# A first stage whose sums go to VectorE and whose first panel runs chunk by chunk, and third panels split earlier

## What is computed

```python
for l in range(DEPTH):
    mod = silu_c @ w_ada[l] + b_ada[l]
    sh_a, sc_a, g_a, sh_f, sc_f, g_f = jnp.split(mod[:, None, :], 6, axis=-1)
    ...
    hx = rmsnorm(x) * (1 + sc_a) + sh_a
    hc = rmsnorm(ctx) * (1 + mc[1]) + mc[0]
    ux = hx @ w_in[l]
    ...
    x = x + g_a * (jnp.concatenate([fx, ax, rx], axis=-1) @ w_out[l])
    x = x + g_f * swiglu(rmsnorm(x) * (1 + sc_f) + sh_f, w_gate[l], w_up[l], w_down[l])
```

## Time and profile before

| | |
|---|---|
| runs of the kernel before, us | 3932.67, 3937.05, 3923.95 (median 3932.67) |
| the profiled execution, its own time | 3933.46 us |
| its span in the profile | 3932.2 us |
| mean granted TensorE clock | 0.96 |
| PE busy | 3710.9 us (94%) |
| DVE busy | 1800.4 us (46%) |
| ACT busy | 1170.1 us (30%) |
| line 389, low halves of 260 panels, DVE | 595.2 us, 2291 ns each |
| line 384, high halves of 260 panels, ACT | 495.3 us, 1907 ns each |
| from main memory | 335.95 MB, 86 GB/s over the span |

### The profile page before, as it was taken

One profiled execution on the slowest core, in us unless ns is written; L12 is line 12 of the kernel. 1 busy time (PEld: TensorE's weight loads), 2 busy tenths in 40 slices (PEclk: granted clock), 3 DMA queues, 4 the chain that ended last, 5 costly groups with the idle time before them and its releaser, 6 DMA issues.

```text
span 3932.2 us, 46910 instructions
## 1 busy us (share of the span) xinstructions
PE 3710.9 (94%) x20048; PEld 3027.0 (77%) x20048; DVE 1800.4 (46%) x2365; ACT 1170.1 (30%) x1511; POOL 144.3 (4%) x122
## 2 busy tenths in 40 slices
PE   7989889999999888999999999799999999999998
PEld 5866678888887566788788877578887888777886
DVE  3125655222243367433454456654446445466444
ACT  3125333111132253322332233442223223223222
POOL 1000210000000012000000002000000000000000
PEclk9999799999999998999999999899999999999999
DMA  6414201111111100222322222022222222222221
GB/s 246 161 71 162 88 33 55 64 65 65 65 65 65 71 3 31 89 97 97 118 86 97 97 97 73 26 96 97 97 98 96 97 97 107 86 86 78 99 98 59
DMA packets 47757, 341.06 MB, mean 87 GB/s; under 512 B 5392, under 2 KB 5552, under 8 KB 7744
## 3 DMA queue, kind: packets, MB, share of 16 engines
q1 hardware_dynamic: 41184, 301.09, 21.3%
q0 software_dynamic: 5216, 34.88, 2.3%
q10 hardware_dynamic: 1152, 2.10, 0.1%
HBM read 335.95 MB, written 2.10 MB: 86 GB/s over the span
## 4 chain that ended last, share of the span: by engine, by line
PE 88%; DVE 6%; ACT 2%; issue 2%; POOL 1%; DMA 1%; DVEq 0%; ACTq 0%; POOLq 0%
PE PS L412 52%; PE PS L430 18%; PE PS L414 7%; PE PS L1038 2%; PE PS L1054 1%; PE PS L1093 1%; DVE nmax_a L1188 1%; PE PS L1335 1%; PE PS L516 1%; DVE SQ L553 1%; PE PS L713 1%; PE PS L1068 1%; PE PS L1626 1%; PE PS L505 0%; PE PS L644 0%
## 5 line engine op out<-in xcount | busy, mean ns | idle before, releaser
L389 DVE TENSOR_TENSOR WL<-raw,WH 128x2048 fp32r<-128x2048 f32 x260 | 595.2, 2291 | 299.9 <-ACT WH L384 299.8
L384 ACT ACTIVATE WH<-raw 128x2048 fp32r<-128x2048 f32 x260 | 495.3, 1907 | 575.3 <-PE PS L412 346.6
L412 PE MATMUL PS<-XH_ff,WH 128*128 128x512 f32 x640 | 254.3, 397 | 6.9 <-DVE WL L389 6.9
L412 PE MATMUL PS<-XL_ff,WH 128*128 128x512 f32 x640 | 252.3, 394 | 0.0
L412 PE MATMUL PS<-XH_ff,WL 128*128 128x512 f32 x640 | 251.4, 393 | 0.0
L2024 DVE TENSOR_TENSOR GA_ff<-PS,GA_ff 128x512 f32<-128x512 f32 (+1 forms) x63 | 36.0, 599 | 334.5 <-PE PS L414 222.4
L412 PE MATMUL PS<-XH_a,WH 128*128 128x512 f32 x448 | 174.3, 389 | 0.0
L412 PE MATMUL PS<-XL_a,WH 128*128 128x512 f32 x448 | 174.3, 389 | 0.0
L412 PE MATMUL PS<-XH_a,WL 128*128 128x512 f32 x448 | 174.3, 389 | 0.0
L412 PE MATMUL PS<-XH_b,WH 128*128 128x512 f32 x448 | 174.3, 389 | 0.0
L412 PE MATMUL PS<-XL_b,WH 128*128 128x512 f32 x448 | 174.3, 389 | 0.0
(11 more groups left out here) (414 smaller groups left out, 8377.4 us busy)
## 6 DMA issues: line engine op xcount, KB each, us to landing
raw<-in_panels SPq DMA_DIRECT2D x260, 1024.0 KB, 4.7
ada_at<-in_ada_panels SPq DMA_DIRECT2D x24, 1024.0 KB, 4.8
ada_win<-in_ada_panels POOLq DMA_DIRECT2D x18, 1024.0 KB, 5.1
ada_start<-in_ada_panels POOLq DMA_DIRECT2D x6, 1024.0 KB, 22.5
FX<-in_dft_x POOLq DMA_DIRECT2D x2, 2048.0 KB, 8.2
X<-in_xT SPq DMA_DIRECT2D x1, 3072.0 KB, 11.2
out<-X ACTq DMA_DIRECT2D x8, 256.0 KB, 2.0
rope<-in_rope POOLq DMA_DIRECT2D x2, 768.0 KB, 10.2
```

Source lines behind the costliest of these rows:

```text
L384: H.up(ac.activation(WH[s].rearrange("p k n -> p (k n)"), raw[:, n % 2, :], ACT.Copy), n)
L389: L.up(ve.tensor_tensor(WL[s].rearrange("p k n -> p (k n)"), raw[:, n % 2, :], WH[s].bitcast(F32).rearrange("p k n -> p (k n)"), ALU.subtr ...
L412: t = te.matmul(PS[:, j, :], lhsT, x[:, k, 0:SEQ], start=st, stop=end)
```

## The change

It has three parts.

1. **The start.** Raw panel 0 is asked for first, then X in four transfers of two chunks each, then raw panel 1; POOL asks for the ada panels only when the first quarter of X has landed. ScalarE and VectorE split panel 0 before the squares. The squares are summed on VectorE (`ve_square_sum`) instead of TensorE. TensorE does root, spread and the first four ada panels ahead of panel 0, with the root in bank 0 and the spread in banks 2 and 3. Panel 1 is split behind the root.
2. **Panel 0 chunk by chunk.** `te_first` goes over the chunks k and in each over both blocks; ada panels 4 to 7 of the start stand between the chunks. VectorE's copies and additions for them are spread over the loop of `ve_normed`, which scales chunks 4 and 6 after the low half of the chunk ahead. The sixteen other ada panels are spread over panels 1 to 8.
3. **The entries.** In ff0, wi1 and ff1 the third panel is split right behind the normed chunks, ahead of the first panel's results. The second panel's split stands behind the root. `bias_sum` stands behind `te_root`, at k = 1, and uses bank 4.

The core of the diff (signals, plain renaming of banks and the same edits in the other engines' programs are left out):

```diff
@@ -114,7 +114,7 @@
...
 SPLITS = split_steps()
-ENTERED = entered_stages() | {FIRST["ff0.up0"], FIRST["wi1"], FIRST["ff1.up0"]}
+ENTERED = entered_stages() | {0} | {FIRST[name] + p for name in ("ff0.up0", "wi1", "ff1.up0") for p in range(2)}
...
@@ -366,6 +366,8 @@
...
                 panel_landed[n % 2].up(sp.dma_start(raw[:, n % 2, :], panels[n]), n)
+                if n == 0:
+                    sp_x()
...
@@ -418,6 +420,27 @@
...
                     beside(p, 2)
+        def te_first(name, XH, XL, ready, beside, evac):
+            p0 = FIRST[name]
+            for k in range(NC):
+                beside(k)
+                ready(k)
+                for j in range(2):
+                    if k == 0:
+                        te.wait_ge(*L[p0])
+                        wait_bank(j)
+                        wait_bank(2 + j)
+                    for q, (w, x) in enumerate(((WH, XH), (WH, XL), (WL, XH))):
+                        st, end = k == 0 and q == 0, k == NC - 1 and q == 2
+                        lhsT = w[0][:, k, j * P:(j + 1) * P]
+                        te.matmul(PS[:, j, :], lhsT, x[:, k, 0:SEQ], start=st, stop=end)
+                        t = te.matmul(PS[:, 2 + j, 0:CTX], lhsT, x[:, k, SEQ:TOK], start=st, stop=end)
+                    if k == NC - 1:
+                        B.up(t, (name, j))
+                        evac(j, j)
+            B.mark(("panel", p0))
...
@@ -554,9 +577,10 @@
...
+            late = (4, 6) if ahead else ()
             scale(0)
             for c in range(NC):
-                if c + 1 < NC:
+                if c + 1 < NC and c + 1 not in late:
                     scale(c + 1)
...
@@ -564,6 +588,10 @@
...
                     V.up(t, (name, "XL", c))
+                    if after:
+                        after(c)
+                    if c + 1 in late:
+                        scale(c + 1)
                     if c + 2 < NC:
...
@@ -622,11 +650,10 @@
...
                 te.wait_ge(*A[(name, "bias parts")])
-                wait_bank(5)
                 for j in range(2):
-                    t = te.matmul(PS[:, 5, 2 * j:2 * j + 2], RS[:, j * P:(j + 1) * P], HM[:, 2:4], start=True, stop=True)
+                    t = te.matmul(PS[:, 4, 2 * j:2 * j + 2], RS[:, j * P:(j + 1) * P], HM[:, 2:4], start=True, stop=True)
                 T.up(t, (name, "bias"))
-                bank(5, V, name, "bias")
+                bank(4, V, name, "bias")
...
@@ -654,10 +681,9 @@
...
                 T.up(t, (name, "raw", k))
-                if k == 0:
-                    bias_sum()
                 if k == 1:
                     te_root(name, norm_ctx)
+                    bias_sum()
                 if k == (2 if ctx else 3):
...
@@ -668,22 +694,24 @@
...
             A.up(ac.activation(RS[:, 0:2 * P], PS[:, 4, 0:2 * P], ACT.Copy), (name, "bias parts"))
-            for q in SPLITS[FIRST[run]]:
-                ac_split(q)
-            ac_stats(name, norm_ctx, False)
+            ac_stats(name, norm_ctx, False, between=SPLITS[FIRST[run]])
...
             ac_normed(name, XH, norm_ctx, shift, free)
+            for q in SPLITS[FIRST[run] + 1]:
+                ac_split(q)
         def ve_enter1(name, run, XH, XL, norm_ctx, gain, shift):
+            ve_stats(name, norm_ctx)
             ve.wait_ge(*T[(name, "bias")])
-            V.up(ve.tensor_copy(shb[:], PS[:, 5, 0:4]), (name, "bias"))
-            ve_stats(name, norm_ctx)
+            V.up(ve.tensor_copy(shb[:], PS[:, 4, 0:4]), (name, "bias"))
             for q in SPLITS[FIRST[run]]:
...
             ve_normed(name, XH, XL, norm_ctx, gain, shift)
+            for q in SPLITS[FIRST[run] + 1]:
+                ve_split(q)
...
@@ -752,39 +780,39 @@
...
         ada_use = {}
-        plans = {2: ("P0", "S0 P1", "S1 P2", "S2 P3", "S3")}
-        def ada_steps(start, rounds, p, j):
-            x = 2 * (p % 2) + j
-            if (j == 2 and x != 4) or p // 2 >= 4:
+        def ada_steps(p, j):
+            x = 2 * p + j - 2
+            if p == 0 or j == 2:
                 return []
-            return [(what[0], int(what[1]), start + (p // 2) * 2 * rounds + int(what[1]))
-                    for what in plans[rounds][x].split()]
-        def te_ada(name, b, start, rounds):
+            if x == 0:
+                return [("P", 0), ("P", 1)]
+            if x == 1:
+                return [("S", 0), ("S", 1), ("P", 2)]
+            return [("S", x)] + ([("P", x + 1)] if x + 1 < MOD // 2 - NC else [])
...
@@ -798,67 +826,118 @@
...
             cvec_landed.up(sp.dma_start(cv[:], cvec))
-            x_landed.up(sp.dma_start(X[:, :, :], xT))
+        def sp_x():
+            for i in range(4):
+                x_landed[i].up(sp.dma_start(X[:, 2 * i:2 * i + 2, :], xT[:, 2 * i:2 * i + 2, :]))
...
             const_landed.up(gp.dma_start(HM[:], head_mask), "all")
+            gp.wait_ge(*x_landed[0].now())
             for s, panel in enumerate(START):
...
             A.up(ac.activation(cv[:], cv[:], ACT.Silu), "cv")
+            ac_split(0)
             ac.wait_ge(*A["cv"])
             A.up(ac.activation(sh[:], cv[:], ACT.Copy, scale=0.0))
-            ac.wait_ge(*x_landed.now())
             ac.wait_ge(*V["consts"])
             for c in range(NC):
-                if c >= 2:
-                    ac.wait_ge(*T[("wi0", "sum", c - 2)])
-                A.up(ac.activation(SQ[c % 2][:, 0:TOK], X[:, c, :], ACT.Square), ("wi0", "square", c))
-            ac_stats("wi0", True, True)
+                if c % 2 == 0:
+                    ac.wait_ge(*x_landed[c // 2].now())
+                if c >= 3:
+                    ac.wait_ge(*V[("wi0", "square", c - 2, "added")])
+                A.up(ac.activation((SQ[c % 2] if c else SS)[:], X[:, c, :], ACT.Square), ("wi0", "square", c))
+            ac_stats("wi0", True, False, RS, 0, 2, SPLITS[0])
...
             V.up(ve.memset(one[:], 1.0), "consts")
+            ve_split(0)
+            for c in range(1, NC):
+                ve_square_sum("wi0", ("wi0", "square", c), c % 2, TOK, c == 1)
+            ve_stats("wi0", True)
+            ve_start_copy(0)
+            ve_start_copy(1)
             ve.wait_ge(*const_landed["all"])
-            for s in range(2):
-                ve_ada_parts("st", START[s], mix1[0]["AD"], s)
-            ve_stats("wi0", True)
-        def ve_start_chunks(c):
+            ve_start_bias(0)
+            ve_start_bias(1)
+            for q in SPLITS[0]:
+                ve_split(q)
+            ve_start_copy(2)
+            ve_start_copy(3)
+            ve_start_bias(2)
+            ve_start_bias(3)
+        def ve_start_copy(s):
+            ve_ada_parts("st", START[s], mix1[0]["AD"], s)
+        def ve_start_bias(s):
+            ve_ada_bias("st", START[s], s)
+        def ve_start_scale(c):
+            if c == 4:
+                ve_start_bias(5)
+            if c == 6:
+                ve_start_bias(7)
             if c % 2 == 0:
-                for s in (c, c + 1):
-                    ve_ada_bias("st", START[s], s)
-                for s in (c + 2, c + 3):
-                    if s < NC:
-                        ve_ada_parts("st", START[s], mix1[0]["AD"], s)
-                ve.wait_ge(*V.now())
+                ve.wait_ge(*V[("st", "mods")])
+        def ve_start_split(c):
+            if c == 1:
+                ve_start_copy(4)
+            if c == 2:
+                ve_start_copy(5)
+                ve_start_bias(4)
+            if c == 3:
+                ve_start_copy(6)
+            if c == 4:
+                ve_start_copy(7)
+                ve_start_bias(6)
+        def te_start_parts(s):
+            te_ada_parts("st", START[s], ring_start[s], start_landed[s], s)
+            bank(4 + s % 2, V, "st", "parts", START[s])
+        def te_start_sum(s):
+            te_ada_sum("st", START[s], mix1[0]["AD"], s, V)
         def te_start():
+            te.wait_ge(*V["consts"])
+            te_root("wi0", True, False, 0)
+            te.wait_ge(*A["cv"])
+            te_start_parts(0)
+            te_start_parts(1)
             te.wait_ge(*const_landed["all"])
-            te.wait_ge(*V["consts"])
-            for c in range(NC):
-                te_sum("wi0", c, True)
-            bank(6, A, "wi0", "SS")
-            bank(7, A, "wi0", "SS")
-            te.wait_ge(*A["cv"])
-            def parts(s):
-                te_ada_parts("st", START[s], ring_start[s], start_landed[s], s)
-                bank(4 + s % 2, V, "st", "parts", START[s])
-            parts(0)
-            parts(1)
-            te_stats("wi0", True, True)
-            for s in range(NC):
-                te_ada_sum("st", START[s], mix1[0]["AD"], s, V)
-                if s % 2:
-                    for x in (s + 1, s + 2):
-                        if x < NC:
-                            parts(x)
+            te_start_sum(0)
+            te_start_sum(1)
+            te_start_parts(2)
+            te_spread_root("wi0", True, False, 2)
+            te_start_parts(3)
+            te_start_sum(2)
```

(22 more changed lines are left out.)

66 lines of the change are left out of this document (33 added, 33 removed).

## The result

The changed kernel takes 3913.82 us (median of 11 runs, 3900.27 to 3923.58) against 3932.67 for 11 runs of the kernel before: ratio 0.9939, interval 0.9925 to 0.9953, so by the ratio 24 us or 0.6% faster; the two medians lie 18.9 us apart. The profiled execution took 3902.7 us with a span of 3901.4, 30.8 us less than that of before (3932.2). That is more than the change is worth, as the table shows. Each row is a difference of marks that both traces have.

The account below looks back on a forecast made before the run. The chain that ended last was 88% TensorE, so only its waits, half clock or excess work counted. Start 8.6, ff0 2.0, wi1 7.5 and ff1 5.7 sum to 23.8 us: 3933.46 to 3909.7, range 3899 to 3923.

Parts of the forecast that it names:

- X has landed at 18: Start: with panel 0 loaded first and the queues sharing the rate, X's last quarter lands near 18 us.
- The sum at 20.5: Start: two squares and an add, 2.7 us, follow X's last quarter; the sum of squares is ready near 20.5.
- First scaling at 34.0: Start: VectorE first scales X at 34.0 against 42.19; 32 at full clock, 37 with half clock throughout.
- Panel 0 at 64.2: First projection: panel 0, done chunk by chunk, ends at 64.2 us against 75.74.
- The ada work moved out: First projection: two ada parts and a sum now come after panel 0, costing 2.9 us; the start gives 8.6.
- ff0, 2.0: First feed-forward: moving the third panel's split ahead removes all of TensorE's 2.03 us wait, gaining 2.0 us.
- ff1, 5.7: Last entry: TensorE starts the third panel 4.2 us earlier and avoids 1.5 of half clock, together 5.7 us.
- wi1, 7.5: Second projection: first scaling 6.6 us earlier if the clock stays full, 0.9 off the third panel's wait, together 7.5.
- My first rival: Second projection's half clock does not recover; wi1 gives 3.4 us, total 3913.8; chance 0.14.
- A starved POOL queue: Start: ada loads issued late beside VectorE's adds, start gives nothing; chance 0.03, within 0.13 for a poor start.
- The evacuations: Entries: waits for evacuations replace those for the split in wi1 and ff1; 13 us remain, 3920; chance 0.08.
- Slower: Panel 0: ada part 7, expected at 52 us, comes late ahead of chunk 4; slower from 76 on; chance 0.05.

Follow-up runs that it names:

- e4_before_again: The kernel before, run once more unaltered: 3934.47 us, ratio 0.9983 to the kernel before.
- e6_bias: The kernel before with only the bias sum behind the root and the second panel's split behind it: 3930.04 us.
- e11_after_third: The changed kernel, unaltered, a third time: 3914.64 us, ratio 0.9936 to the kernel before.
- e1_entries: The kernel before with part 3 of the change alone (the entries): 3918.97 us, ratio 0.9947.
- e2_start: The changed kernel with part 3 undone, so parts 1 and 2 alone: 3923.91 us, ratio 0.9960 to the kernel before.
- e7_nohold: The changed kernel without GpSimd's wait for the first quarter of X before the ada loads: 3906.82 us, a single execution.
- e8_blocks: The changed kernel with panel 0 in whole blocks and the ada steps ahead of it: 3928.75 us, a single execution.
- e9_early_x: The changed kernel with X loaded ahead of raw panel 1 and the ada panels, panel 1 split later: 3908.27 us, ratio 0.9923 to the kernel before.

## Why the prediction was right, step by step

*X has landed at 18*: right, 18.4 to 18.8 in the three profiles of the changed kernel. The shared rate sets it: without the hold it is 22.5.

*The sum at 20.5*: 21.7. Most of that is X's last quarter, 0.8 later than the 18 taken. From it to the sum 2.9 us pass, where two squares and an add were put at 2.7 (and 18 and 2.7 are 20.7).

*First scaling at 34.0*: 34.3 and 34.0, by luck in part, since the mixture was wrong. I had TensorE mostly at full clock and the fourth ada panel at 30 as the limit. The panel was there (TensorE waits for no ada load between 22 and 35), and the half clock lasted some 6 us. In the third profile it lasted 14, and the scaling came at 37.2, the value that I had given as the end for half clock throughout. So the bound was right, and I should have seen that the term is a draw within one kernel: 34.0 to 37.2.

*Panel 0 at 64.2*: it was done at 65.4, where its second evacuation starts. Of the 1.2 us, 0.3 is the later scaling, 0.4 lies between the first matmul and chunk 4 (16.6 us for 14.1 and 2.1) and 0.5 behind it (11.0 for 10.5). The steps between were right to a few tenths: 3.5 us to the first matmul, a first chunk at half clock, a wait of 0.30 for chunk 4, from whose low half the rest was counted, and one of 1.58 for chunk 6 (forecast 1.6). *The ada work moved out*, 2.9 us: the evacuation of the whole projection is 159.95 us behind the first panel's (225.39 - 65.44); before, it was 157.3 behind the start of panel 1 (233.06 - 75.74). That is 2.6 us more. Together 7.7 for 8.6; with the third profile it is 4.3.

*ff0, 2.0*: 2.16, all by the split. In `e4_before_again` and `e6_bias` half clock behind the wait adds 1.7 to what the wait costs, which the forecast didn't have. *ff1, 5.7*: 5.95, and by single steps too: TensorE starts 4.55 us earlier (4.2), the rest is the clock (1.5). In the other three profiles with the old entry the clock costs 2.8 instead of 1.4, so the change gives 7.4 there. The 0.5 us that I left for the fourth panel held. *The second panel's split behind the root puts the scaling back*: by 0.31 in ff0 (0.1 expected) and by 0.03 in ff1 (0.3 expected), hidden in ff0.

*wi1, 7.5*: 7.4 in the pair of profiles on which I built it, with the wait cut from 2.68 to 1.89 (0.8, forecast 0.9). As a statement about the kernels it was too sure. The term had 4.8 us in it that the kernel before loses at this place in some executions only; against one that keeps its clock there it is 2.6, and 4.1 with the half clock behind the third panel's wait. My first rival had it the wrong way round: I asked if the new order would get the clock back, which it had in ten profiles of ten, and not if the old one always lost it. That the sum of the three entries came out all the same (15.2 forecast; 15.9, 15.3 and 17.1 in three profiles with the old entries, counted to the end of the third panel) is luck in part: what was too much in wi1 was left out behind the waits of ff0 and ff1. The Trainium skill says in "TensorE: Matmul & The Clock Gate", section "What's actually happening", that the gate is free-running and its point of change moves between runs; the kernel before agrees, with +18.18, +16.63, +13.43 and +13.40 for the same instructions behind the same wait of 1.5 us.

*The other rivals.* A starved POOL queue didn't appear. The ada panels were asked for from 10.1 on, while VectorE added squares, and TensorE waited for none of them. The delay that I had taken from the Trainium skill ("SBUF — State Buffer", section "SBUF: two separate sides") did not show beside these adds and this split. The page speaks of operations in a two-port mode; that the adds or the split run in one, no run here shows, so this says nothing against the page. The evacuations do take the place of the split in wi1 and ff1, as that rival says, but with 1.89 and 0.28 us instead of all. Its sum was wrong as put: start, ff0 and half of the rest are 17 us and not 13. *Slower*: the matmul of ada panel 7 came at 52.58, forecast 52, and TensorE's wait before its chunk is 0.30.

*The total.* The sum of the marks is 23.2 us in the profiled pair; the ratio of the runs gives 24 and their medians 18.9. For the three sets of runs of the changed kernel the ratios give 24, 31 and 25 us and the medians 18.9, 29.0 and 22.1. So the total bears the forecast out within some 7 us, and that the terms are right is shown by the marks, not by it. The profiled execution is 7.6 us better than the marks, and the rows of the table without a forecast are the reason. The largest is TensorE's pace in ff0. The next two are the mixer stages, whose length goes with the granted clock in them: those of layer 1 took 270.4 us at 0.89 in the first profile of the kernel before, 275.0 at 0.86 after, and 283.7 at 0.83 in both `e4_before_again` and `e11_after_third`. The fourteen profiles have 372 to 378 us for layer 0 and 270 to 284 for layer 1, with no order by kernel. The last row goes with the clock too: from 2400 to 2900 us it is 0.95 before and 0.97 after. The three profiles of the changed kernel have spans of 3901.4, 3904.9 and 3926.2 us. Between the first and the last, 10 us are pace in ff0, 3.4 us the start, and 8.8 and 1.9 us the mixers of layers 1 and 0.

What stays open is what sets the pace. It changes at some pause of TensorE and then holds for a whole dense stretch: in the first profile of the kernel before, the output projection ran at 0.3533, the first two panels of ff0 at 0.3467, and the other panels at 0.3533; in its second profile all of these ran at 0.3467. It is not the chip: three chips that were profiled more than once (`e1_entries` and `e2_start`; `e7_nohold` and `e8_blocks`; `e9_early_x` and `e11_after_third`) showed both. It was not tried to set it. Open too is what puts half clock behind one wait and not behind another of the same length.

## What to carry to other kernels

Work that one engine does for a later need, such as splitting the next weight panel, goes ahead of the evacuation of results only where the buffer of these results isn't asked for first: here the pair of waits was 4.82 us for the split and 0.28 us for the evacuation. When a small step stands behind another engine's copy (here a bias sum), put work between that is ready, even where the wait is only 1.5 us: in two of four profiles a half-clock stretch followed it that cost two to three times as much, and in ten profiles without the wait none did. Before a term that rests on a half-clock stretch enters a sum, look at a second profile of the same kernel: here the stretch stood behind the bias sum in two of four, and the executions that lacked it had others behind the waits that came later.
